# Load of a value unit's second half, issued by ScalarE instead of SyncE

## The chip, the cores and the metric

One core of a Trainium2 chip. The time is the device time of one execution in microseconds (us), as median of the runs shown; lower is better.

## The reference

One decoder layer on x of 256 rows by 1024 columns, float32, with two kinds of attention side by side:

```python
h = rms_norm(x, norm_pre_g)
proj = einsum('bsd,de->bse', h, w_in)        # w_in: 1024 x (8 * 512 + 8)
q_a, k_a, v_a, g_a, f_a, q_b, k_b, v_b, g_b = split(proj)
y_a = merge_heads(fox_attention(q_a, k_a, v_a, log_sigmoid(f_a + b))) * silu(g_a)
y_b = merge_heads(moba_attention(q_b, k_b, v_b, slopes)) * silu(g_b)
y = einsum('bse,ed->bsd', concatenate([y_a, y_b]), w_out)
out = x + rms_norm(y, norm_post_g)
```

Each kind has 8 heads of 64. `fox_attention` adds a bias from the running sum of the forget gates (`f_a`) to its causal logits; `moba_attention`, with one block for 256 rows, is causal attention with a slope by distance.

## The kernel before

**Precision.** Every float32 operand of a large product is split into two parts that TensorE multiplies in its `fp32r` form: ScalarE writes the high part (a copy rounded to `fp32r`), VectorE the low part (the difference). A product is three passes, high by high, high by low and low by high (`PASSES`, `V_PASSES`).

**Weights** come in units of 128 rows by 1024 columns, 512 KB. `RING = 4` of them have room in `raw` (as loaded) and in `w` (high and low). Units 0 to 7 are value units: unit u is one block of 128 input columns against all 1024 value columns, half of them (`va`) from one array unit and half (`vb`) from another, plus 8 forget columns that GpSimd copies in from `wf` (line 289). Units 8 to 15 are gate units, then queries and keys in turn. The rounding of a unit is `unit_high` (line 380, ScalarE) and `unit_low` (line 615, VectorE); its products are line 947 for values and 937 for the others. Gate unit `V_UNITS + s` waits for its low part and, from `s = 2`, for the gate product (line 680, VectorE) of the unit two before it, whose PSUM bank it takes.

**The beginning.** To let TensorE start early, the first three value units are cut (`PIECES`): unit 0 into columns 0 to 256, 256 to 512, 512 to 768 and 768 to 1032, units 1 and 2 into two halves. Each piece is rounded (line 411), its low part made (line 633) and multiplied on its own. The loads of unit 0 are three: 0 to 256 and 256 to 512 with 128 KB each, and 512 to 1024 with 256 KB, which lands for the last two pieces and is counted by the semaphore `s_raw_in[0]`. TensorE does eight products on ones (line 986) until the first piece is there. x comes transposed in column blocks (`x_t`, line 208), multiplied with `g_pre` and split by lines 398 (ScalarE) and 622 (VectorE).

**Who issues.** SyncE issues nearly all loads, in one order, on its DMA queue (q1 in the trace): x block 0, the three loads of unit 0, x block 1, the two halves of unit 1, then x block and unit for units 2 and 3; from unit 4 on each load first waits until the unit that had its place in the ring is rounded (`sp.wait_ge(s_lo, ...)`). Ahead of units 6 and 7, where no x block is left, x comes once more by rows (line 244, `x_rows`, in the tile named `h`), for the mean squares (line 394, ScalarE): two blocks of 128 rows. From them come `ms`, `root`, `rstd` (lines 424, 640 to 647), a load of another activation table (line 425) and the rounding of units 7 on. ScalarE's own DMA queue (q10) has few transfers; at the start `g_pre` (4 KB, line 387) and `w_f` (32 KB, line 390).

```python
for c, (lo, hi) in enumerate(X_LOADS):
    act.wait_ge(s_x_in[c], 16)
    for j in range(lo, hi):
        x_high(j)
    if c < PIECED:
        for lo, hi in PIECES[c]:
            last = hi == V_WIDTH
            act.wait_ge(s_raw_in[c] if lo >= HALF or c == 2 else s_piece_in[2 * c + lo // SEQ], 16)
            if last:
                act.wait_ge(s_wf, c + 1)
```

Of the kernel before, what the change touches and what calls it, by code (L numbers as in the profile page):

```python
# [27 lines left out]
D_MODEL = 1024  # L28
# [7 lines left out]
HALF = D_MODEL // 2  # L36
UNIT = 1024
V_UNITS = KT
# [25 lines left out]
def hybrid_layer(nc, xt, x, g_pre, w_units, w_f, f_bias, w_out, g_post, out):  # L64
    ctx = ExitStack()

    def sb(name, shape, dt=F32):
        return ctx.enter_context(nc.sbuf_tensor(name, shape, dt))

    def sem(name):  # L70
        return ctx.enter_context(nc.semaphore(name))
# [4 lines left out]
    with ctx:  # L76
# [10 lines left out]
        raw = sb("raw", [P, RING, V_PITCH])  # L87
# [71 lines left out]
        s_raw_in = [sem(f"raw_in{s}") for s in range(RING)]  # L159
# [43 lines left out]
        @block.sync  # L203
        def _(sp):

            def load_x(c):
                lo, hi = X_LOADS[c]
                sp.dma_start(x_t[:, lo:hi, :], xt[:, lo:hi, :]).then_inc(s_x_in[c], 16)

            def load_values(u, lo, hi, landed):  # L210

                part = slice(u % 2 * HALF + lo % HALF, u % 2 * HALF + (hi - 1) % HALF + 1)
                units = slice(lo // HALF * (V_UNITS // 2) + u // 2, V_UNITS, V_UNITS // 2)
                n = 1 if hi <= HALF else 2 - lo // HALF
                sp.dma_start(raw[:, u % RING, lo:hi].rearrange("p (a c) -> p a c", a=n),
                             w_units[units, :, part][0:n].rearrange("a p c -> p a c")).then_inc(landed, 16)

            load_x(0)
            load_values(0, 0, SEQ, s_piece_in[0])
            load_values(0, SEQ, HALF, s_piece_in[1])  # L220
            load_values(0, HALF, D_MODEL, s_raw_in[0])
            load_x(1)
            load_values(1, 0, HALF, s_piece_in[2])
            load_values(1, HALF, D_MODEL, s_raw_in[1])
            for u in range(2, RING):
                load_x(u)
                load_values(u, 0, D_MODEL, s_raw_in[u])

            def load_unit(r, s):

                sp.wait_ge(s_lo, r * RING + s + 1 - RING)
                sp.dma_start(raw[:, s, 0:UNIT], w_units[r * RING + s]).then_inc(s_raw_in[s], 16)

            def load_out_unit(j):
                if j > 1:
                    sp.wait_ge(s_olo, j - 1)
                sp.dma_start(raw_out[j % 2], w_out[j]).then_inc(s_raw_out_in[j % 2], 16)

            for u in range(RING, V_UNITS):
                if u < len(X_LOADS):  # L240
                    load_x(u)
                else:
                    t = u - len(X_LOADS)
                    sp.dma_start(x_rows[:, t, :], x[:, t, :]).then_inc(s_xrows_in[t], 16)
                sp.wait_ge(s_lo, u + 1 - RING)
                load_values(u, 0, D_MODEL, s_raw_in[u % RING])
            sp.dma_start(fb_row[:, :], f_bias.rearrange("h o -> o h").to_broadcast((P, HEADS))).then_inc(s_fb_in, 16)

            for u in range(V_UNITS, QK_0 + 2 * RING):
                load_unit(u // RING, u % RING)  # L250
                if u in OUT_BEHIND:
                    load_out_unit(OUT_BEHIND.index(u))


            for i in range(1, PAIRS + 1):
                for u in range(QK_0 + 6 + 2 * i, QK_0 + 8 + 2 * i):
                    if u < UNITS:
                        load_unit(u // RING, u % RING)
                    elif u < UNITS + RING:
                        sp.wait_ge(s_lo, u + 1 - RING)  # L260
                        sp.dma_start(raw[:, u % RING, 0:UNIT], w_out[OUT_OWN + u - UNITS]).then_inc(s_raw_in[u % RING], 16)
            sp.wait_ge(s_olo, OUT_OWN)
            sp.dma_start(gpost_row[:, :], g_post[0:1, :].to_broadcast((P, D_MODEL))).then_inc(s_gpost_in, 16)
            sp.wait_ge(s_h32, KT)
            sp.dma_start(x_nat, x).then_inc(s_xnat_in, 16)
            for t, c in ((0, 0), (0, 1), (1, 0)):
                sp.wait_ge(s_fin[t][c], 1)
                sp.dma_start(out[t, :, c * HALF:(c + 1) * HALF],
                             x_nat[:, t, c * HALF:(c + 1) * HALF]).then_inc(s_stored, 16)
            sp.wait_ge(s_last, 1)  # L270
            sp.dma_start(out[1, :, HALF + SEQ:], x_nat[:, 1, HALF + SEQ:]).then_inc(s_stored, 16)
            sp.wait_ge(s_stored, 16 * (2 * TT + 1))
# [100 lines left out]
        def _(act):  # L373
# [11 lines left out]


            act.dma_start(gpre_col[:, :], g_pre).then_inc(s_g_in, 16)
            act.wait_ge(s_ones, 1)
            nc.scalar.activation(root[:, 0:1], ones[:, 0:1], ACT.Sqrt).then_inc(s_table, 1)
            act.dma_start(wf[:, :, :], w_f).then_inc(s_wf_in, 16)  # L390
# [821 lines left out]
```

## Time and profile before

| | |
|---|---|
| runs | 144.88, 145.12, 145.19 us, median 145.12 |
| profiled execution | 145.13 us |
| its span, first to last instruction | 143.3 us |
| granted TensorE clock, mean | 0.992 |
| busy: TensorE, VectorE, ScalarE, GpSimd | 94%, 76%, 69%, 28% of the span |
| DMA moved | 26.96 MB, 188 GB/s over the span |

The profile is of one execution. Its time stands beside its span, since 1.8 us lie around the first and last instruction. Engines: PE is TensorE, PEld its weight loads, DVE VectorE, ACT ScalarE, POOL GpSimd, SP SyncE; a q behind the name (SPq, ACTq) is the engine's instruction queue, which issues DMAs. A share of busy time is a mean over stages with different limits: what one wait costs has to be read at its place.

### The profile page before, as it was taken

To read this page: it belongs to the slowest core of one execution; us is meant where nothing else is said; L and a number is where in the kernel's file an instruction comes from. 1 tells how busy PE (TensorE), PEld (TensorE's weight loads), DVE (VectorE), ACT (ScalarE), POOL (GpSimd) and SP (SyncE) were. 2 spreads that over 40 slices of the span, in tenths; PEclk is the share of its full clock that TensorE was granted. 3 is DMA by queue.
4 is the path that set the end of the run, shared out by engine and by line. 5 is a ranking of instruction groups with operands and counts; after the bars stand their busy time and mean duration, and the time that the engine had idled before them with its cause. 6 is when DMAs were issued, how large, how long until landed. Compare 5 with 4: busy or idle time off the path is not lost.

```text
span 143.3 us, 2857 instructions
## 1 busy us (share of the span) xinstructions
PE 134.4 (94%) x1076; PEld 127.4 (89%) x1076; DVE 109.4 (76%) x230; ACT 98.7 (69%) x198; POOL 40.0 (28%) x58
## 2 busy tenths in 40 slices
PE   7789999999999999999999999999999999999910
PEld 7679999999999999999999999999998888988910
DVE  0384966899999999988888977999689816471891
ACT  4376989678976398977875977778879833355740
POOL 3621100000000067000599235230735551120042
PEclk9999999999999999999999999999999999999996
DMA  4999999398865999758368603449600000000034
GB/s 110 233 313 386 401 395 342 88 375 254 271 223 172 389 392 377 278 160 238 112 230 237 213 9 142 146 166 293 280 2 0 0 0 5 0 0 0 0 149 146
DMA packets 9725, 26.96 MB, mean 188 GB/s; under 512 B 1384, under 2 KB 2416, under 8 KB 9456
## 3 DMA queue, kind: packets, MB, share of 16 engines
q1 hardware_dynamic: 9120, 25.57, 52.0%
q10 hardware_dynamic: 592, 1.22, 2.3%
q8 instruction: 8, 0.13, 0.4%
q14 instruction: 5, 0.04, 0.1%
HBM read 25.73 MB, written 1.06 MB: 187 GB/s over the span
## 4 chain that ended last, share of the span: by engine, by line
PE 87%; DMA 4%; issue 2%; DVE 2%; ACT 1%; POOL 1%; SPq 1%; POOLq 1%; DVEq 0%; ACTq 0%
PE bank L937 47%; PE score_banks L947 11%; PE bank L1128 7%; PE score_banks L1128 5%; PE score_banks L1033 4%; PE value_banks L947 4%; DMA raw<-in_w_units 4%; PE value_banks L1056 1%; PE value_banks L1044 1%; PE value_banks L1060 1%; PE value_banks L1045 1%; POOL x_t L366 1%; DVE h L882 1%; PE bank L1046 1%; PE value_banks L1059 1%
## 5 line engine op out<-in xcount | busy, mean ns | idle before, releaser
L615 DVE TENSOR_TENSOR w_lo<-raw,w_hi 128x1024 fp32r<-128x1024 f32 (+1 forms) x33 | 44.6, 1353 | 6.6 <-ACT w_hi L380 6.5
L380 ACT ACTIVATE w_hi<-raw 128x1024 fp32r<-128x1024 f32 (+1 forms) x33 | 34.4, 1056 | 6.5 <-DMA raw<-in_w_units 4.1
L937 PE MATMUL bank<-h_hi,w_hi 128*128 128x256 f32 x128 | 36.0, 281 | 0.0
L937 PE MATMUL bank<-h_lo,w_hi 128*128 128x256 f32 x128 | 35.6, 278 | 0.0
L937 PE MATMUL bank<-h_hi,w_lo 128*128 128x256 f32 x128 | 35.5, 278 | 0.0
L937 PEld LDWEIGHTS bank<-h_hi,w_hi 128*128 128x128 f32 x128 | 24.1, 188 | 0.4
L937 PEld LDWEIGHTS bank<-h_lo,w_hi 128*128 128x128 f32 x128 | 24.0, 188 | 0.0
L937 PEld LDWEIGHTS bank<-h_hi,w_lo 128*128 128x128 f32 x128 | 24.0, 188 | 0.0
L334 POOL TENSOR_TENSOR probs<-probs,row_inv 128x256 f32<-128x256 f32 (+1 forms) x16 | 15.7, 1005 | 27.6 <-DVE row_inv L764 27.5
L937 PE MATMUL bank<-xg_hi,w_hi 128*128 128x256 f32 x64 | 17.8, 278 | 0.0
L937 PE MATMUL bank<-xg_lo,w_hi 128*128 128x256 f32 x64 | 17.7, 277 | 0.0
L937 PE MATMUL bank<-xg_hi,w_lo 128*128 128x256 f32 x64 | 17.7, 276 | 0.0
L326 POOL TENSOR_TENSOR bias<-squares,causal 128x256 f32<-128x256 f32 x4 | 6.3, 1573 | 35.1 <-DMA squares<-decay_rows_scratch 35.1
L477 ACT ACTIVATE probs<-probs,neg_max 128x128 f32<-128x128 f32 (+1 forms) x32 | 14.1, 448 | 0.3 <-DVE neg_max L757 0.3
L937 PEld LDWEIGHTS bank<-xg_hi,w_hi 128*128 128x128 f32 x64 | 12.0, 188 | 0.0
L937 PEld LDWEIGHTS bank<-xg_lo,w_hi 128*128 128x128 f32 x64 | 12.0, 188 | 0.0
L937 PEld LDWEIGHTS bank<-xg_hi,w_lo 128*128 128x128 f32 x64 | 12.0, 188 | 0.0
L947 PE MATMUL score_banks<-w_hi,xg_hi 128*128 128x512 f32 (+2 forms) x34 | 8.8, 336 | 1.4 <-ACT w_hi L411 1.4
L947 PE MATMUL score_banks<-w_lo,xg_hi 128*128 128x512 f32 (+2 forms) x34 | 8.7, 330 | 0.0
L339 POOL TENSOR_TENSOR xg_lo<-y_parts,xg_hi 128x512 fp32r<-128x512 f32 x3 | 5.3, 1772 | 11.6 <-ACT xg_hi L488 11.6
L947 PE MATMUL score_banks<-w_hi,xg_lo 128*128 128x512 f32 (+2 forms) x34 | 8.5, 328 | 0.0
L947 PEld LDWEIGHTS score_banks<-w_hi,xg_hi 128*128 128x128 f32 x34 | 5.8, 188 | 2.0 <-ACT w_hi L411 1.6
(172 smaller groups left out, 326.5 us busy)
## 6 DMA issues: line engine op xcount, KB each, us to landing
raw<-in_w_units SPq DMA_DIRECT2D x30, 512.0 KB, 4.8
raw<-in_w_out SPq DMA_DIRECT2D x4, 512.0 KB, 3.2
h<-in_x SPq DMA_DIRECT2D x2, 512.0 KB, 8.1
y_parts<-in_w_out SPq DMA_DIRECT2D x2, 512.0 KB, 5.6
gpost_row<-in_w_out SPq DMA_DIRECT2D x2, 512.0 KB, 6.1
squares<-decay_rows_scratch ACTq DMA_DIRECT2D x1, 1024.0 KB, 5.9
x_t<-in_x SPq DMA_DIRECT2D x1, 1024.0 KB, 7.1
raw<-in_w_units SPq DMA_DIRECT2D x3, 256.0 KB, 5.2
```

What stands on the lines that cost most here:

```text
L326: pool.tensor_tensor(bias[:, own, :], decay[:, heads, 0:P], mask, ALU.add).then_inc(s_bias, 1)
L334: pool.tensor_tensor(own, own, row_inv[:, 4 * b + t:4 * b + 4:2].unsqueeze(2).to_broadcast((P, 2, hi - lo)), ALU.mult).then_inc(s_norm, 1)
L339: pool.tensor_tensor(y[1][:, 2 * d:2 * d + 2, :], y32[:, :, :], y[0][:, 2 * d:2 * d + 2, :].bitcast(F32), ALU.subtract).then_inc(s_ylo, 1)
L366: pool.tensor_tensor(x_nat[:, 0, HALF:], x_nat[:, 0, HALF:], y_post[:, 0, HALF:], ALU.add).then_inc(s_fin[0][1], 1)
L380: nc.scalar.activation(w[0][:, s, 0:width], raw[:, s, 0:width], ACT.Copy).then_inc(s_hi, 1)
L477: nc.scalar.activation(own, own, ACT.Exp, bias=neg_max[:, c:c + 1], scale=-1.0, accum_out=row_sum[:, c:c + 1]).then_inc(s_exp, 1)
L615: nc.vector.tensor_tensor(w[1][:, s, 0:width], raw[:, s, 0:width], w[0][:, s, 0:width].bitcast(F32), ALU.subtract).then_inc(s_lo, 1)
L882: nc.vector.tensor_tensor(kept, group, gpost_row[:, cols], ALU.mult).then_inc(s_ypost, 1)
L937: last = nc.tensor.matmul(dst, stationary(a, j), moving(b, j), start=n == 1, stop=n == count * len(PASSES))
L947: last = nc.tensor.matmul(v_banks[t][c][:, lo - first:hi - first], xg[a][:, u, t * P:(t + 1) * P], w[b][:, u % RING, lo:hi], start=u == 0 ...
L1033: last = nc.tensor.matmul(s_ps[:, 2 * (i % 2) + a, lo:hi], q[x][own, i % 4, t * P:(t + 1) * P], k[z][own, i % 2, 0:hi - lo], start=n == 0, ...
L1128: last = nc.tensor.matmul(dst, y[a][:, p, t * P:(t + 1) * P], wide, start=p == 0 and (a, b) == PASSES[0], stop=p == PAIRS - 1 and (a, b) = ...
```

## The change

The load of columns 512 to 1024 of value unit 0 leaves SyncE's list and stands in ScalarE's program, directly behind `g_pre`'s. Source, destination and semaphore stay the same.

```diff
@@ -218,7 +218,6 @@
             load_x(0)
             load_values(0, 0, SEQ, s_piece_in[0])
             load_values(0, SEQ, HALF, s_piece_in[1])
-            load_values(0, HALF, D_MODEL, s_raw_in[0])
             load_x(1)
             load_values(1, 0, HALF, s_piece_in[2])
             load_values(1, HALF, D_MODEL, s_raw_in[1])
@@ -385,6 +384,7 @@
 
 
             act.dma_start(gpre_col[:, :], g_pre).then_inc(s_g_in, 16)
+            act.dma_start(raw[:, 0, HALF:D_MODEL], w_units[V_UNITS // 2, :, 0:HALF]).then_inc(s_raw_in[0], 16)
             act.wait_ge(s_ones, 1)
             nc.scalar.activation(root[:, 0:1], ones[:, 0:1], ACT.Sqrt).then_inc(s_table, 1)
             act.dma_start(wf[:, :, :], w_f).then_inc(s_wf_in, 16)
```

SyncE's first instructions, before (`raw` is the ring of weights, 128x256 and 128x512 are pieces of it; `x_t` is transposed x):

```order
L208 DMA x_t<-in_xt 128x256
L215 DMA raw<-in_w_units 128x256 x2
L215 DMA raw<-in_w_units 128x512
L208 DMA x_t<-in_xt 128x256
L215 DMA raw<-in_w_units 128x512 x2
```

and with the change:

```order
L208 DMA x_t<-in_xt 128x256
L215 DMA raw<-in_w_units 128x256 x2
L208 DMA x_t<-in_xt 128x256
L215 DMA raw<-in_w_units 128x512 x2
```

One load is gone from between the two small pieces and x's second block. ScalarE's first instructions, before (`root<-ones` is the activation that brings the first table):

```order
L387 DMA gpre_col<-in_g_pre 128x8
L389 ACT_TABLE_LOAD
L389 ACTIVATE root<-ones 128x1
L390 DMA wf<-in_w_f 128x64
L398 ACTIVATE xg_hi<-x_t,gpre_col 128x256
```

and with the change (a line less in the code above moves `g_pre` to line 386):

```order
L386 DMA gpre_col<-in_g_pre 128x8
L387 DMA raw<-in_w_units 128x512
L389 ACT_TABLE_LOAD
L389 ACTIVATE root<-ones 128x1
L390 DMA wf<-in_w_f 128x64
L398 ACTIVATE xg_hi<-x_t,gpre_col 128x256
```

The load stands between `g_pre`'s and the table load, and ahead of `w_f`'s on the same queue. TensorE, VectorE and GpSimd keep their instructions and order.

## Rows read from the trace of the kernel before

**Rows 1.** Waits of TensorE: engine, line, waited for: us, times, longest.

```profile
PE score_banks L947 <- ACT w_hi L411: 1.4, 1, 1.4
PE bank L986 <- POOL ones L291: 1.0, 1, 1.0
```

**Rows 2.** Chain of waits, 0 to 40 us: start, us, what.

```profile
0.75 0.38 SPq L208
1.19 0.42 SPq L215
1.66 0.42 SPq L215
2.12 5.16 DMA raw<-in_w_units
7.31 0.42 ACT w_hi L411
7.78 0.38 PE score_banks L947
```

**Rows 3.** Timeline, 0 to 14 us: start, us, engine, line, what [idle before, ended by].

```profile
1.20 1.28 ACT L389 ACT_TABLE_LOAD   x1 [1.20 <-PEq L1205]
...
3.71 0.51 ACT L398 ACTIVATE xg_hi<-x_t,gpre_col 128x256 fp32r<-128x256 f32 x1 [1.02 <-DMA gpre_col<-in_g_pre]
...
4.21 0.99 POOL L289 COPY raw<-wf 128x8 f32<-128x8 f32 x4 [2.34 <-DMA wf<-in_w_f]
...
6.01 0.40 PE L947 MATMUL score_banks<-w_lo,xg_hi 128*128 128x256 f32 x2
...
7.78 0.38 PE L947 MATMUL score_banks<-w_hi,xg_hi 128*128 128x256 f32 x1 [1.36 <-ACT w_hi L411]
...
8.34 1.26 ACT L411 ACTIVATE w_hi<-raw 128x512 fp32r<-128x512 f32 x2
...
9.31 0.63 PE L947 MATMUL score_banks<-w_hi,xg_hi 128*128 128x512 f32 x2
```

**Rows 4.** DMA, first 3.5 us: packets by queue; issues, count, KB each, us to landing.

```profile
q1 hardware_dynamic: 371, 0.34, 33.2%
q10 hardware_dynamic: 277, 0.03, 6.4%
...
raw<-in_w_units SPq DMA_DIRECT2D x2, 128.0 KB, 2.8
wf<-in_w_f ACTq DMA_DIRECT2D x1, 32.0 KB, 2.9
```

**Rows 5.** Windows: us, busy of PE, PEld, DVE, ACT, POOL, clock, DMA share, GB/s.

```profile
2.00:4.00 2.00, 2.00 (x12) 2.00 (x11) 0.00 (x0) 0.97 (x3) 0.00 (x0) 1.00 0.79 205
4.00:6.00 2.00, 2.00 (x14) 1.82 (x14) 1.15 (x3) 0.83 (x3) 1.74 (x14) 1.00 0.89 213
6.00:8.00 2.00, 0.64 (x6) 0.43 (x4) 0.24 (x1) 0.69 (x3) 0.67 (x3) 1.00 0.96 285
8.00:14.00 6.00, 6.00 (x40) 5.46 (x40) 4.40 (x9) 4.08 (x9) 1.18 (x3) 1.00 1.01 359
14.00:21.50 7.50, 7.50 (x52) 6.91 (x51) 5.52 (x8) 6.51 (x11) 0.38 (x1) 1.00 1.05 398
25.48:46.60 21.12, 21.12 (x179) 20.75 (x179) 20.98 (x38) 15.80 (x22) 0.00 (x0) 1.00 0.70 232
```

**Rows 6.** Timeline at unit 3, 13 to 15 us.

```profile
13.48 1.07 ACT L380 ACTIVATE w_hi<-raw 128x1032 fp32r<-128x1032 f32 x1 [1.14 <-DMA raw<-in_w_units]
...
14.96 0.39 PE L947 MATMUL score_banks<-w_hi,xg_hi 128*128 128x512 f32 x1
```

**Rows 7.** Timeline, ScalarE, VectorE and TensorE, 21 to 41 us.

```profile
21.48 1.06 ACT L394 ACTIVATE squares<-h 128x1024 f32<-128x1024 f32 x1 [0.26 <-DMA h<-in_x]
...
25.48 2.37 DVE L615 TENSOR_TENSOR w_lo<-raw,w_hi 128x1032 fp32r<-128x1032 f32 x2 [0.90 <-ACT w_hi L380]
...
29.53 0.28 PE L937 MATMUL bank<-xg_hi,w_hi 128*128 128x256 f32 x1
...
37.08 0.42 DVE L680 TENSOR_TENSOR gate<-bank,rrow 128x256 f32<-128x256 f32 x1
...
39.68 0.42 DVE L680 TENSOR_TENSOR gate<-bank,rrow 128x256 f32<-128x256 f32 x1
...
40.43 0.38 PE L1016 MATMUL score_banks<-ident,forget 128*8 128x128 f32 x2
40.56 0.37 PE L937 MATMUL bank<-xg_hi,w_hi 128*128 128x256 f32 x1
```

**Rows 8.** DMA, issue at 13.2 us: KB, us to landing.

```profile
h<-in_x SPq DMA_DIRECT2D x1, 512.0 KB, 8.3
```

## The prediction

> **What bounds the kernel now.** I read the waits of TensorE first, since it is busy for 94% of the span. It has two idle stretches in the whole program [rows 1]: 1.0 us at the start, before anything can run, and 1.4 us for ScalarE's `w_hi`, the high half of a weight. Everything else on TensorE follows back to back, and what stands behind its last product is a fixed tail. So the change can give at most those 1.36 us, and only as far as nothing later takes them back.
>
> The chain of waits shows where the 1.36 us come from [rows 2]. SyncE issues x's first column block and then three pieces of value unit 0. The third, its second half (512 columns, 256 KB), is issued at 2.12 and has landed 5.16 us later, at 7.28. ScalarE rounds it from 7.31, TensorE starts on it at 7.78. The timeline [rows 3] shows the two sides of the hole: the last product of the first two pieces begins at 6.01, and the one at 7.78 has an idle time of 1.36 before it.
>
> **What the change does to that load.** ScalarE's queue now holds `g_pre` (issue 0.75), the half, and `w_f`. `g_pre`'s issue ends and ScalarE's table load starts at 1.20 [rows 3], so the half is issued at about 1.2 instead of 2.12: 0.9 earlier. SyncE loses one issue of 0.46 (its issues follow each other at that distance, 1.19, 1.66, 2.12) [rows 2], so x's second block and all that follows is issued 0.46 earlier.
>
> When does the half land? Upper bound: it takes 5.16 again, 6.4. Lower bound: 2.8, as a 128 KB piece just ahead of it took [rows 4], 4.0; it is larger and shares the engines with the others, so I take 5.7, between them. Either way TensorE, done with the first pieces near 6.4, could go on by 6.9 at the latest (6.4, plus 0.42 of ScalarE and 0.1 of hand-over). So **up to 0.9 to 1.36 us are offered here**.
>
> **What pays for it.** (a) x's first block and the first two pieces share the DMA engines with 256 KB more. At the full rate of [rows 5], 398 GB/s, those are 0.66 us. TensorE would finish the first pieces at 7.1 at worst, which is inside the hole: nothing. (b) The activation table load moves from 1.20 to 1.65. ScalarE waits 1.02 us for `g_pre` behind it [rows 3], so nothing. (c) `w_f` now comes behind 256 KB in one queue. It landed 2.9 after its issue; now it lands with the half. GpSimd needs 0.25 for the first of four copies (0.99 together) [rows 3], ScalarE 0.32 for the third piece before it wants them: 0 to 0.1. GpSimd's later work moves back by as much as `w_f` (4.2 to about 5.8, 1.6 us); its next copies are wanted for units 2, 3 and 4, the first of them by ScalarE at about 11 and unit 3's at 13.48 [rows 6]. The copies for units 0 to 3 are one run of 0.99, so this is hidden too.
>
> **What takes it back.** This decides the size. Next to be late are things that the DMA engines deliver, not what the moved load frees.
>
> Unit 1: its first half is rounded from 8.34 in two activations of 1.26 together, so the first is ready at 8.97; TensorE uses it at 9.31 [rows 3]. Room: 0.34, less 0.05 of hand-over (rounding ends at 7.73, product at 7.78), 0.29.
>
> Unit 3: rounded from 13.48 to 14.55 directly on its landing, used at 14.96 [rows 6]. Room 0.41 - 0.05 = 0.36.
>
> Gate unit 11 (the fourth): four gate units run from 29.53 to 40.43, so 2.72 each, and the fourth starts at 37.70. It waits for two VectorE steps, the low half of its weight and the gate product of unit 9. That product runs at 37.08 and ends at 37.50 [rows 7]. Room 0.20 - 0.05 = **0.15**. VectorE is busy for 20.98 of the 21.12 us from 25.48 on [rows 5], so this time isn't set by TensorE but by when VectorE began. That was set by ScalarE's table load and the rounding of unit 7, behind the square sums of x's second row block, which started on a landing (idle 0.26, "DMA h<-in_x") at 21.48 [rows 7]. The fifth gate unit has 0.46 - 0.05 = 0.41 in the same way (product ends at 40.10, used at 40.56) [rows 7].
>
> So TensorE can gain no more than 0.15 plus what the landing of x's second row block is pulled forward; call that d. The DMA engines' share [rows 5] bounds d. From 8 us on they are full (1.01, 1.05): an earlier issue there is worth nothing, since x's second row block takes 8.3 us from issue to landing anyway [rows 8]. Only time in which they idled can be won: in 2 to 4 us the share is 0.79, so 0.42 us idle, about SyncE's 0.46 of issue time. Upper end d = 0.42. Lower end d = 0, if the slowest of the sixteen engines, which sets each landing, had no idle time. Below that it could fall, because the share counts slow packets as work: 213 GB/s at a share of 0.89 in 4 to 6 us, against 398 at 1.05 later. Nothing in the trace says that a second queue makes those better or worse. I take d = 0.2, the middle.
>
> **Sum.** Gain 0.15 + 0.2 = 0.35 us, the other 0.55 or more turning into short waits of TensorE at unit 1, unit 3 or the gates. The profiled execution took 145.13, the median is 145.12, so nothing is corrected: **144.8 us**. About 0.2% (0.29 us) is what a measurement can tell from no change.
>
> Does a second queue add anything? The rows show the two queues' packets side by side in the first 3.5 us (371 of q1, 277 of q10) [rows 4]. The Trainium skill, "DMA: Bandwidth & Descriptors", section "Issuing engines are not separate DMA queues", says that DMAs started from different engines run on the same 16 DMA engines and interleave, so that only the sequencer's time to start them is saved. The trace agrees as far as it goes. By that rule, where the engines are full, the sum would be 0.15 alone.
>
> **Rivals.**
>
> 1. *No pull-in (d near 0).* The half lands early, but every later landing keeps its time since the bytes ahead are the same. For: the shares of 1.01 and 1.05 [rows 5] and the 8.3 us [rows 8]. Against: the 0.79 at the start. TensorE starts early and gives all but 0.15 back at gate unit 11: 144.97, within noise. This is also what the rule of the Trainium skill gives.
> 2. *More than that.* The slow packets of 4 to 6 us overlap across two queues. 213 GB/s instead of the 285 of the next two microseconds leaves 0.14 MB behind, 0.4 us at 359 GB/s. Then d = 0.2 + 0.4, gain 0.75, 144.4. Unit 1 and unit 3 must be pulled along.
> 3. *The other side.* Two queues taking turns prolong the slow phase, or push one engine further behind; x's second row block lands later. The price at 213 instead of 359 GB/s is 0.4 us for each microsecond that the slow phase grows. It decides from 0.15 us on, the room at gate unit 11. With 1.5 us of growth: d = -0.6, 0.45 slower, 145.6.
> 4. *The change doesn't do what it says.* The half is held up on the slow engines and lands at 7.3 as before, since it was not the issue but the packets that were late. For: 5.16 against 2.8 for an issue 0.46 before it. TensorE starts at 7.78: 145.1.
>
> **Chances.** Forecast (d from 0.14 to 0.42) 0.45; rival 1 (d within 0.14 of zero, gain 0.01 to 0.29) 0.32; rival 2 0.08; rival 3 0.10; rival 4 0.05. Faster by over 0.2% are forecast and rival 2, less what touches the bound: 0.50. Within: rivals 1 and 4 and the small end of 3: 0.41. Slower: 0.09. Range: from rival 2, 144.3, over forecast and rival 1 to a small case of rival 3, 145.3. The forecast's own range, d from 0.14 to 0.42, is 144.55 to 144.85.
>
> **What would show it.** The half's landing before 6.5, and the hole before its first product at 0.5 us or less. New short waits of TensorE, for ScalarE at unit 1 or 3, or for VectorE at the fourth gate unit, 0.5 us or more in sum. x's second row block starting its squares at about 21.3 instead of 21.48, and VectorE's run at 25.3 instead of 25.48. The prediction is wrong if that squares row moves by more than 0.5 either way, if TensorE has no new wait although it began a microsecond earlier, or if the first pieces' products end after 7.8. If squares and run move but the time doesn't, it is the argument on gate unit 11 that failed.

## The result and the profile after

| | before | with the change |
|---|---|---|
| median of 22 runs each | 145.31 us | 146.76 us |
| ratio, 95% interval | | 1.0055, 1.0033 to 1.0078 |
| profiled execution, its span | 145.13, 143.3 | 146.74, 144.9 |

The change makes the kernel slower, by 0.55% (0.33% to 0.78%), where 0.35 us faster was forecast. The ratios, here and below, leave out executions of over 1.5% above a kernel's fastest, 10 of 22 with the change and 2 of 22 before, which is why the medians are further apart (1.45 us, 1.0%) than this ratio. Each ratio below is against executions of the kernel before taken beside that version; their medians are 145.16 to 145.33.

The waits of TensorE in the changed kernel name the same pair as [rows 1], 0.4 us longer:

```profile
PE score_banks L947 <- ACT w_hi L411: 1.8, 1, 1.8
PE bank L986 <- POOL ones L290: 1.0, 1, 1.0
```

But it is another hole. The chain of waits, against [rows 2]:

```profile
0.75 0.38 SPq L208
1.18 4.82 DMA raw<-in_w_units
6.03 0.43 ACT w_hi L411
...
6.59 3.11 PE score_banks L947 x13
```

The load in the chain is no longer the one that was moved, it is SyncE's second: value unit 0's **first piece**, 128 KB, issued at 1.18 as ever and landed at 6.00 instead of 3.99. (3.99 is the earliest of four traces with SyncE's old list: in those of experiments 2 and 7, where only the number of products on ones differs, it is 4.53, 4.67 and 4.82. So the piece is 1.2 to 2.0 us later.) The moved half did land earlier, at about 6.6 instead of 7.3 (issue 1.20, 5.4 us), but nobody waits for it. The timeline, against [rows 3]:

```profile
6.03 0.42 ACT L411 ACTIVATE w_hi<-raw 128x256 fp32r<-128x256 f32 x1 [2.21 <-DMA raw<-in_w_units]
...
6.59 0.77 PE L947 MATMUL score_banks<-w_hi,xg_hi 128*128 128x256 f32 x2 [1.81 <-ACT w_hi L411]
...
7.15 1.04 POOL L288 COPY raw<-wf 128x8 f32<-128x8 f32 x4 [5.28 <-DMA wf<-in_w_f]
7.15 0.63 PE L947 MATMUL score_banks<-w_hi,xg_lo 128*128 128x256 f32 x2
...
7.58 0.63 PE L947 MATMUL score_banks<-w_lo,xg_hi 128*128 128x256 f32 x2
...
8.00 0.63 PE L947 MATMUL score_banks<-w_hi,xg_hi 128*128 128x256 f32 x2
...
10.22 0.28 PE L947 MATMUL score_banks<-w_hi,xg_hi 128*128 128x264 f32 x1
...
10.34 0.28 PE L947 MATMUL value_banks<-w_hi,xg_hi 128*128 128x264 f32 x1
...
10.95 0.62 PE L947 MATMUL score_banks<-w_hi,xg_hi 128*128 128x512 f32 x2
```

Two things are to be seen. The hole of 1.36 ahead of the half is gone, and one of 1.81 stands ahead of the first product, which begins at 6.59, not 4.67. And from 7.15 on, pairs of products of 256 columns follow each other every 0.43, so 0.213 each; from 9.9 on it is 0.12, TensorE's usual pace here. 256 columns in 0.213 us are one column per cycle at 1.2 GHz, the lower of the clock's two levels. The views print a granted clock of 1.00 for this stretch, but the trace has no record of the clock before 9.77: there the first one begins, and it is of the upper level, 2.4 GHz. In the kernel before, the first record begins at 4.43, while TensorE is still at the products on ones. So in this trace TensorE went into its real work at the lower level, and 1.00 printed ahead of the first record says nothing. Thirteen such steps lie between 6.94 and 9.71 (three in the kernel before) and cost 1.2 us. Unit 1 begins at 10.95 instead of 9.31, 1.64 later, and the execution takes 1.61 more. The first gate product, at 29.53 before [rows 7], is at

```profile
31.15 0.28 PE L937 MATMUL bank<-xg_hi,w_hi 128*128 128x256 f32 x1
```

From there to the end of the execution it takes 115.6 us in both kernels (145.13 - 29.53, 146.74 - 31.15), and 115.50 to 115.77 in all 20 traces. So all but 0.3 us of any difference is made before it.

The windows, against [rows 5]:

```profile
2.00:4.00 2.00, 2.00 (x12) 2.00 (x11) 0.08 (x1) 1.67 (x3) 0.00 (x0) 1.00 0.77 158
4.00:6.00 2.00, 0.78 (x4) 0.48 (x3) 0.41 (x1) 0.00 (x0) 0.00 (x0) 1.00 0.85 258
6.00:8.00 2.00, 1.41 (x6) 1.44 (x7) 1.05 (x3) 1.49 (x5) 0.85 (x4) 1.00 1.03 350
```

158 GB/s in 2 to 4 us instead of 205, at nearly the same share of busy time. The phase of slow packets, in which the engines are busy and deliver little, is not longer than before; it has moved forward. Before, it lay behind the first pieces (213 GB/s in 4 to 6). Now it lies on them, as it comes with the half.

### The profile page after: what moved, and what is told of

Read it like the earlier page. It is cut to its first block, busy times and chain, and to the rows that moved or that the text cites. A ratio compares the mean times of both kernels' runs of the same rounds, so it can differ in the third digit from the quotient of the medians.

```text
span 144.9 us, 2857 instructions
## 1 busy us (share of the span) xinstructions
PE 135.6 (94%) x1076; PEld 128.7 (89%) x1076; DVE 109.8 (76%) x230; ACT 98.6 (68%) x198; POOL 41.2 (28%) x58
## 4 chain that ended last, share of the span: by engine, by line
PE 88%; DMA 3%; issue 2%; DVE 2%; ACT 1%; POOL 1%; POOLq 1%; SPq 0%; DVEq 0%; ACTq 0%
PE bank L937 46%; PE score_banks L947 13%; PE bank L1128 7%; PE score_banks L1128 5%; PE score_banks L1033 4%; PE value_banks L947 4%; DMA raw<-in_w_units 3%; PE value_banks L1056 1%; PE value_banks L1044 1%; PE value_banks L1060 1%; PE value_banks L1045 1%; POOL x_t L365 1%; DVE h L882 1%; PE bank L1046 1%; PE value_banks L1059 1%
## 5 line engine op out<-in xcount | busy, mean ns | idle before, releaser
L325 POOL TENSOR_TENSOR bias<-squares,causal 128x256 f32<-128x256 f32 x4 | 6.9, 1737 | 36.7 <-DMA squares<-decay_rows_scratch 36.7
L947 PE MATMUL score_banks<-w_hi,xg_hi 128*128 128x512 f32 (+2 forms) x34 | 9.4, 354 | 1.8 <-ACT w_hi L411 1.8
L947 PE MATMUL score_banks<-w_hi,xg_lo 128*128 128x512 f32 (+2 forms) x34 | 9.0, 345 | 0.0
L947 PEld LDWEIGHTS score_banks<-w_hi,xg_hi 128*128 128x128 f32 x34 | 6.3, 208 | 2.4 <-issue 2.1
```

Of the source, the lines that this page charges most:

```text
L325: pool.tensor_tensor(bias[:, own, :], decay[:, heads, 0:P], mask, ALU.add).then_inc(s_bias, 1)
L947: last = nc.tensor.matmul(v_banks[t][c][:, lo - first:hi - first], xg[a][:, u, t * P:(t + 1) * P], w[b][:, u % RING, lo:hi], start=u == 0 ...
```

## Experiments

**1. A second trace of the change.**

> The changed kernel once more, as a second trace. Theory F (the first piece pays): value unit 0's first piece, which landed at 3.99 before and at 6.00 in the changed kernel's trace, lands late again, above 5.0; TensorE's hole stands ahead of line 947's first product, and behind a hole of over about 1.5 us its products of 256 columns follow each other at 0.21 us instead of 0.12 for some 3 us. Time 145.5 to 147. Rival N (chance): the first trace caught an odd execution, the slow packets at 2.9 to 3.9 us are not the change's, and here the first piece lands by 4.5 and the time is 145.2 or less.

Median 146.02, ratio 1.0038 (1.0006 to 1.0071), profiled 145.75. The first piece lands at 6.09, the half at 6.86, so theory F is right on the landing. On the pace it is not: the products keep 0.12 behind a hole of 1.89, and the record of the upper clock level begins at 5.49, ahead of them:

```profile
6.67 0.47 PE L947 MATMUL score_banks<-w_hi,xg_hi 128*128 128x256 f32 x2 [1.89 <-ACT w_hi L411]
6.99 0.40 PE L947 MATMUL score_banks<-w_hi,xg_lo 128*128 128x256 f32 x2
7.22 0.40 PE L947 MATMUL score_banks<-w_lo,xg_hi 128*128 128x256 f32 x2
```

This splits the 1.61 us of the first trace: 0.6 for the late first piece (145.75 against 145.13; the first product comes 2.0 later and the hole of 1.36 is gone), 1.0 for the half pace, which this execution did not have. How many of the others had it isn't known, since only two were traced.

**2. Longer warm-up.** `-WARM_UP = 8` `+WARM_UP = 14`, on the changed kernel and on the one before.

> The changed kernel with 14 instead of 8 products on ones, so that TensorE is busy until about 6.2. Theory F with the clock: the first piece lands as late as in the changed kernel (5 to 6), but its products run at 0.12 from the start, so that unit 1 begins about 1.4 us earlier than in the changed kernel: time within 0.3 of the kernel before. Rival L (only the late landing costs, the pace of the products is not the hole's doing): the time is that of the changed kernel, 146 to 146.8, or later by what the products on ones overrun.

> The control: the kernel before with 14 products on ones. They end near 6.1 instead of 4.67 and delay the first two pieces, whose products (1.4 us at the fast pace) then end near 7.6, still ahead of the second half's first product at 7.78. Both theories: no change, 145.0 to 145.5. If it is slower by more than 0.3, the products on ones cost by themselves and the run above has to be read against this one.

Medians 145.61 (ratio 1.0027, 1.0010 to 1.0044) and 145.51 (1.0025, 1.0006 to 1.0044). The products on ones ran to 7.16 and 7.07, later than the 6.2 I had written: I had taken them to double their pace early, and they keep 0.21 until the upper clock level is on record, from 6.84 and 6.66 (the last of them are 0.11 apart). So they overran the first piece in both (first product at 6.92 and 6.83), no hole is left, and with it the two kernels are alike, though the first piece lands at 5.86 in one and 4.53 in the other. The changed kernel's spread shrinks from 144.8 to 148.8 to 145.1 to 145.9 (one of 230 us left out). The late landing alone, with TensorE kept busy until it, costs nothing that shows.

**3. The contention alone.** In the kernel before:

```diff
             act.dma_start(gpre_col[:, :], g_pre).then_inc(s_g_in, 16)
+            act.dma_start(gate[:, 0:2, :].rearrange("p a n -> p (a n)"), w_units[V_UNITS // 2, :, 0:HALF]).then_inc(s_extra, 16)
...
+            dve.wait_ge(s_extra, 16)
             gate_product(V_UNITS)
```

> The kernel before, with its second half loaded by SyncE as ever, and the same 256 KB loaded a second time by ScalarE behind g_pre's load into a tile that is not in use yet (the extra data is used for nothing). It measures the contention alone. Theory F: the first piece lands at 5 to 6 as in the changed kernel although SyncE's list is untouched, and the time is at least that of the changed kernel, 146 to 148 (0.25 MB more ahead of all others is 0.66 us at 398 GB/s). Rival S (the changed kernel is late because SyncE's later loads start 0.46 earlier and crowd the first pieces, not because of ScalarE's load): the first piece lands near 4.0 and the time is 145.1 to 145.8.

Median 146.97, ratio 1.0064 (1.0024 to 1.0104); first piece at 6.15. SyncE's list is that of the kernel before, so its earlier issues are not to blame. Rival S falls. This trace also shows the half pace beside a clock record. The products are 0.21 apart from 7.68 to 11.11, and the granted clock, last but two in the row, is at 0.50, the lower level:

```profile
7.70:11.10 3.40, 3.40 (x17) 3.40 (x17) 3.04 (x7) 2.69 (x6) 3.18 (x16) 0.50 1.04 384
```

Here the upper level was on record from 4.25, and it fell at 7.66: TensorE had been idle from 4.58 to 6.74 and busy again for 0.9 us.

**4. The same bytes ahead, on SyncE's own queue.** `load_values(0, HALF, D_MODEL, s_raw_in[0])` moved up, behind `load_x(0)`.

> The second half on SyncE's queue as before, but ahead of the first two pieces, so that the same bytes are in front of them with no second queue. Theory B (bytes and slow packets: whatever stands in front of or beside the first piece delays it): the first piece lands at 5.0 to 6.2, as in the changed kernel (6.0), and the time is 145.6 to 147. Rival Q (two queues taking turns are what is slow): the first piece is late only by the 256 KB at 398 GB/s and one issue, 0.66 + 0.46, so at about 5.1 or below with no packets of over 0.3 us in front, and the time stays within 0.4 of the kernel before.

Median 146.46, ratio 1.0059 (1.0016 to 1.0103). Half at 4.70, first piece at 5.78, a hole of 1.58. It isn't the second queue: one queue makes the first piece as late. But the profiled execution took 145.03, no longer than the kernel before's: its upper clock level is on record from 4.82 and no product is at half pace. Three of the ten took 144.9 to 145.1, five 146.4 to 147.0. So a late first piece of itself costs between nothing (here) and 0.6 us (experiment 1).

**5. Other moments for the moved load.** Behind `w_f`'s issue, and behind the wait for `g_pre`.

> The changed kernel with the second half issued behind w_f's load instead of ahead of it (about 1.6 instead of 1.2). Theory B: its packets start some 0.4 us later, the first piece has fewer of them beside it and lands at 4.5 to 5.5, the second one still late; hole ahead of the first piece under 1.5 us, time 145.2 to 146.2, between the two kernels. Rival (any load on the second queue does it): first piece at 6.0 and 146 to 146.8 as in the changed kernel.

> The second half issued by ScalarE only when g_pre has landed (about 3.3), 1.2 us later than SyncE issued it before. Theory B: the first two pieces land at 4.0 and 4.4 as before; the half now competes with x's second block and unit 1 and lands at 7.0 to 8.0; TensorE's hole of 1.4 us stays ahead of the half; time 145.0 to 145.8. Rival: if a queue of its own got the half through in 2.8 us, it would land by 6.2 and the time would be 144.7 to 144.9.

Behind `w_f`: first piece at 4.36, earlier than theory B had it, second piece at 6.25 (4.36 before), half at 6.79, median 145.09, ratio 0.9971 (0.9941 to 1.0001). 0.5 us later at the issue, and the slow packets lie behind the first piece again; most of the loss is gone, though a gain is not certain: eight executions took 144.2 to 145.5, four 146.6 to 147.1. Behind the landing: 147.51, ratio 1.0164 (1.0121 to 1.0206), slower than either theory said, for the half takes 6.2 us and lands at 9.55, with everything else ahead of it or beside it:

```profile
10.04 0.39 PE L947 MATMUL score_banks<-w_hi,xg_hi 128*128 128x256 f32 x1 [3.55 <-ACT w_hi L411]
```

Here a queue of its own gave the load no precedence. The next products follow at 0.12: the upper clock level is on record from 4.85 and stays, even through a hole of 3.55.

**6. The second piece moved instead.** Of the kernel before, `load_values(0, SEQ, HALF, s_piece_in[1])` goes to ScalarE's queue behind `g_pre`, the half stays.

> A version that might beat both: of the kernel before, the second piece (128 KB) goes to ScalarE's queue behind g_pre, the half stays on SyncE's and is issued 0.46 earlier. Theory B: half of the changed kernel's bytes beside the first piece and of 1 KB packets as its own: first piece at 4.3 to 5.2 (hidden up to about 4.4, then TensorE is idle ahead of it), half at 6.8 to 7.3; time 144.8 to 145.5. If the first piece lands at 6, the second queue is to blame at any size.

Median 144.98, ratio 0.9982 (0.9942 to 1.0021): no change that can be told, but its profiled execution is the fastest of the lot, 144.23. First piece at 4.51, half at 6.30. The half came earlier than expected. At the fourth gate unit, where the prediction put its limit, the square sums start at 20.58 (21.48 before), the gate product ends at 36.60, 16.02 later in both kernels, and is used at 36.77:

```profile
36.18 0.42 DVE L680 TENSOR_TENSOR gate<-bank,rrow 128x256 f32<-128x256 f32 x1
...
36.77 0.28 PE L937 MATMUL bank<-xg_hi,w_hi 128*128 128x256 f32 x1
```

TensorE and VectorE both come 0.9 us earlier, so the room stays, 0.17 against 0.20 [rows 7], and the limit isn't reached. But the prediction's upper end for d, 0.42, isn't a general bound: with another load moved the square sums come 0.90 earlier.

**7. The hole without the late landing, and two warm-ups.** `WARM_UP = 4` and `10` in the kernel before, `10` in the version of experiment 6.

> The kernel before with 4 instead of 8 products on ones: they end near 2.9, so TensorE is idle for 1.8 us ahead of the first piece, as in the changed kernel, but every load lands as before. Theory C (such a hole costs by itself, because TensorE's products behind it often run at half pace): landings unchanged (4.0, 7.3), products of 256 columns 0.21 apart for some 2 to 3 us in part of the executions, the runs spread to over 146.5, median 0.3 to 1.2 above the kernel before. Rival (only the landing matters, the first pieces are ready at 4.6 anyway): 145.0 to 145.4, spread as before.

> Control for it: the kernel before with 10 products on ones. They end near 5.4, the first pieces' near 6.8, the hole ahead of the half shrinks from 1.4 to 0.9 to 1.0 us and the half's products start at 7.8 as ever: median within 0.2 of the kernel before. By theory C its slower executions (over 146) become rarer.

> The version with the second piece (not the half) on ScalarE's queue, with 10 products on ones instead of 8. They end near 5.4, the first pieces' products (1.4 us) near 6.8, which is when the half's began in that version's trace (6.80): no hole of over 0.3 us is left. Theory C: no executions with a half pace, so the spread goes and the median is 144.2 to 144.8. Rival: 145.0 with a spread of over 1.5 us as without them.

With 4: median 146.08, ratio 1.0037 (0.9999 to 1.0075), products at half pace from 5.60 to 9.68 in its trace, where the first piece landed at 4.67 and the hole was 2.18; the upper clock level is on record from 9.78 only. Landing, pace, median and spread (to 147.65) are what theory C expected, though the interval of the ratio still touches 1. With 10: 145.60, ratio 1.0012 (0.9973 to 1.0052), three of 12 runs over 146, which is no rarer than without (9 of 35). The second piece with 10: 145.21, ratio 0.998 (0.9944 to 1.0016), spread 1.5, but its half landed at 6.57 and left a hole of 0.73, so it doesn't test what it was meant to. A hole without a late landing can bring the half pace, then; that every long hole does is refuted by experiments 1, 4 and 5.

**8. Which rows are read.** The extra load of experiment 3 again, then with other sources: `w_units[V_UNITS // 2 + 1, :, 0:HALF]` (array unit 5) and `w_out[PAIRS - 1, :, 0:HALF]`.

> As the kernel before with the extra 256 KB load on ScalarE's queue, but its source is w_out's last unit (rows of 4 KB pitch, the same packets of 2 KB) instead of the rows of value unit 0's second half. If the slow packets come from beginning to read those rows of the value weights while the first pieces' are read, the first piece lands at 4.3 to 5.0 and the time is 145.2 to 146. If any 256 KB beside the first pieces brings them, the first piece lands at 5.8 to 6.3 and the time is 146 to 147 as with the first extra load.

> The first extra load (the half's own rows, 256 KB, on ScalarE's queue, the half itself still on SyncE's) once more, on the same chip as the three below. First piece at 5.8 to 6.3 again, 146 to 147. If it lands below 5, the difference to w_out's rows was one of chips or executions.

> The same extra load with rows of array unit 5 instead of 4: 2.5 MB instead of 2 MB behind the rows of the first pieces, same pitch and packet size. Theory A (rows exactly 2 MB apart, read side by side, are what makes the packets slow): first piece at 4.5 to 5.2, as with w_out's rows (4.87), and few packets over 0.25 us between 3 and 4.5 us (5, against 19 with unit 4). Theory V (any rows of that array beside the first pieces): 5.8 or later.

> The extra load from w_out's last unit once more. First piece at 4.6 to 5.2 again. If it lands at 5.8 or later here, its first trace was luck, and bytes beside the first pieces are enough.

From `w_out`'s rows the first piece lands at 4.87 and, again, at 4.56, about where most traces of the kernel before have it (4.53 to 4.82); from unit 4's at 6.15 and 5.72, from unit 5's at 5.65. The issue of the first piece (KB, us to landing) and the window of 3 to 4.5 us, unit 4:

```profile
raw<-in_w_units SPq DMA_DIRECT2D x1, 128.0 KB, 4.5
...
3.00:4.50 1.50, 1.40 (x9) 1.20 (x7) 0.49 (x1) 0.68 (x2) 0.00 (x0) 1.00 0.91 165
```

unit 5:

```profile
3.00:4.50 1.50, 1.50 (x9) 1.49 (x7) 0.48 (x1) 0.68 (x2) 0.00 (x0) 1.00 1.01 185
```

and `w_out`:

```profile
raw<-in_w_units SPq DMA_DIRECT2D x1, 128.0 KB, 3.4
...
3.00:4.50 1.50, 1.50 (x9) 1.49 (x7) 0.48 (x1) 0.68 (x2) 0.00 (x0) 1.00 0.89 310
```

310 GB/s against 165 and 185, for the same 256 KB in the same packets (282 and 177 in the first traces of the two). Theory A as written (exactly 2 MB apart) falls with unit 5; theory V stands for these loads: rows of another unit of the same array beside unit 0's are slow, another array's are not. The times, with 4 to 12 runs each, do not separate these four: 146.97 and 147.07 (unit 4), 146.49 (unit 5), 145.74 and 146.44 (`w_out`), the last two apart by as much as the sources are.

The last of these traces is also the one in which the limit of the prediction acts. The gate product that the fourth gate unit waits for ends at 37.37, and that unit starts 0.05 later:

```profile
36.95 0.41 DVE L682 TENSOR_TENSOR gate<-bank,rrow 128x256 f32<-128x256 f32 x1
...
37.42 0.39 PE L940 MATMUL bank<-xg_hi,w_hi 128*128 128x256 f32 x1
```

TensorE loses 0.15 us there (its products, else 0.11 apart, start at 37.28, 37.42 and 37.65), and from the first gate product to the end it takes 115.77 instead of 115.60.

**9. The changed kernel, the half from an array of its own.** The launch lays a copy of that unit into `w_copy`:

```diff
-            act.dma_start(raw[:, 0, HALF:D_MODEL], w_units[V_UNITS // 2, :, 0:HALF]).then_inc(s_raw_in[0], 16)
+            act.dma_start(raw[:, 0, HALF:D_MODEL], w_copy[:, 0:HALF]).then_inc(s_raw_in[0], 16)
```

> The changed kernel, its second half read from an array of its own that holds a copy of that unit (same pitch of 4 KB, another address). Theory A: the first piece lands at 4.6 to 5.2 instead of 6.0, the half by 5.5 to 6.0; TensorE begins near 5.2 and the time is 144.6 to 145.3 where its products keep their pace. Theory V, or bytes alone: first piece at 6.0, time 145.7 to 146.8 as in the changed kernel.

Median **144.64, ratio 0.9961 (0.9932 to 0.9990)**: faster than the kernel before, with the same move that made it slower. (Eight of 12 executions took 143.9 to 144.8, four 145.7 to 146.3.)

```profile
raw<-in_w_copy ACTq DMA_DIRECT2D x1, 256.0 KB, 4.4
raw<-in_w_units SPq DMA_DIRECT2D x1, 128.0 KB, 4.2
...
3.00:4.50 1.50, 1.50 (x9) 1.47 (x7) 0.48 (x1) 0.68 (x2) 0.00 (x0) 1.00 0.83 289
...
5.99 0.47 PE L947 MATMUL score_banks<-w_hi,xg_hi 128*128 128x256 f32 x2 [1.33 <-ACT w_hi L411]
```

The half lands at 5.62, the first piece at 5.41 (later than the 5.2 expected; it is 4.48 in experiment 10, with the same loads), and the rest is delivered in time: unit 1's first product is at 8.91 instead of 9.31. A further array may also shift where the others lie in memory; that was not looked at.

**10. The own array without the move, and with 11 products on ones.**

> The kernel before, its half read from the array of its own, on SyncE's queue as before. Theory A2 (what is slow is reading two places of the weights' array at once): the half lands earlier than at 7.3, at 5.3 to 6.5, the first piece at 4.0 to 4.5, TensorE's hole of 1.4 shrinks to under 0.5, and the gain is the 0.3 to 0.6 that units 1 and 3 allow: 144.5 to 144.9. If it stays at 145.0 to 145.3, the own array helps only where two queues read side by side, and the moved issue is what brings the 144.64 of the version before.

> The changed kernel with the own array and 11 products on ones, which end near 5.7 instead of 4.7, so that little or no hole is left ahead of the first piece (ready at 5.0 to 6.0). Theory C: the slower executions (over 145.7, 4 of 12 without) go, since they are those whose products run at half pace; median 144.3 to 144.7, spread under 1.2. Rival: the same 144.6 with the same spread, or later by what the products on ones overrun.

Without the move: median 145.78, ratio 1.0021 (0.9994 to 1.0049), not the gain that theory A2 expected. The half lands at 5.70, within its bounds, and TensorE's holes are elsewhere:

```profile
5.21 0.47 PE L947 MATMUL score_banks<-w_hi,xg_hi 128*128 128x256 f32 x2 [0.43 <-ACT w_hi L411]
8.89 0.70 PE L947 MATMUL score_banks<-w_hi,xg_hi 128*128 128x512 f32 x2 [0.59 <-ACT w_hi L411]
10.85 0.39 PE L947 MATMUL score_banks<-w_hi,xg_hi 128*128 128x256 f32 x1 [0.33 <-ACT w_hi L411]
```

The slow phase has moved once more, to unit 1, whose two halves now land at 8.09 and 10.14 (8.28 and 8.94 before): the second of them is the first load that reads array unit 4. In 6.5 to 8 us the engines deliver 102 GB/s (289 before), at a busy share of 0.41:

```profile
6.50:8.00 1.50, 1.50 (x15) 1.50 (x14) 0.88 (x3) 0.36 (x1) 1.13 (x4) 1.00 0.41 102
```

A share of 0.41 is unlike the slow stretches shown so far (0.77 to 1.01): here the engines have few packets in flight. In experiment 9 the same two loads of the same rows land at 7.96 and 8.60, with 280 GB/s in that window. So in these runs the gain took both, the array and the move, and why unit 1 is spared there is open. With 11 products on ones: 144.86, ratio 0.9970 (0.9946 to 0.9994), spread 144.4 to 145.7 instead of 143.9 to 146.3: about as fast (144.3 to 144.7 was expected) and, over 12 runs each, steadier. In its trace there is no hole, and yet

```profile
5.71 0.77 PE L947 MATMUL score_banks<-w_hi,xg_hi 128*128 128x256 f32 x2
6.29 0.63 PE L947 MATMUL score_banks<-w_hi,xg_lo 128*128 128x256 f32 x2
6.71 0.53 PE L947 MATMUL score_banks<-w_lo,xg_hi 128*128 128x256 f32 x2
```

from 6.07 to 6.92 the products are 0.21 apart, directly behind the products on ones. The upper clock level is on record from 6.99. The half pace does not need a hole.

## Why the prediction was wrong

**What bounds the kernel, and what the change offers: right in the main.** The hole of 1.36 us was the half's, the half is issued at 1.20, and in both traces of the change it lands earlier (6.56 and 6.86, forecast 5.7, bounds 4.0 and 6.4, so later than the upper one).

**Part (a) of what pays for it: the step that failed.** It said that the 256 KB beside the first pieces cost 0.66 us at 398 GB/s, that TensorE would finish the first pieces at 7.1 at worst, and that this is free. They cost 1.2 to 2.0 us on the first piece (5.86 to 6.09 in three traces, against 3.99 to 4.82 in four), and TensorE *begins* the first pieces at 6.6. I priced the bytes at the rate of 14 to 21 us, while [rows 5] had 205 to 213 GB/s for just this stretch, and 5.16 us for the half itself against 2.8 for its neighbour [rows 2, 4]. I used both rows, the one to bound d and the other to place the half's landing, and not to ask what the slow packets would do to what stands beside the half. Experiments 3 and 4 show that step alone: the load added or put ahead, 5.7 to 6.2 for the first piece, on either queue. Experiment 8 shows that the bytes alone aren't it: with as many of `w_out`'s rows the first piece (4.87, 4.56) is about where three of the four traces of the kernel before have it (4.53 to 4.82). It goes with the half's rows lying in the array from which the first pieces are read; why those are slow stays open.

**The clock: missing.** No term of the sum had it. In the profiled execution TensorE is at the lower level until 9.77, which costs 1.2 us; in experiment 1 it is at the upper one from 5.49, and the late piece alone costs 0.6. That the late start matters for it is borne out by experiment 2, where without a hole the two kernels are alike (145.61 and 145.51).

**(b) and (c): right.** The table load and GpSimd's copies ended nothing that was waited for: the copies ran from 7.15, and ScalarE wanted the first after its third piece, some 0.3 later. `w_f` itself was later than forecast, at 7.09 and not with a half at 5.7.

**What takes it back: not reached, so not tested here.** d was forecast as 0.2 with ends 0 and 0.42; the square sums of x's second row block start at

```profile
21.20 1.06 ACT L394 ACTIVATE squares<-h 128x1024 f32<-128x1024 f32 x1 [0.21 <-DMA h<-in_x]
```

0.28 earlier. That is no more than chance: it is 21.43 in experiment 1, and 21.08 to 21.63 in the kernel before with 4, 10 and 14 products on ones. In the changed kernel TensorE came 1.6 us late to all of it. That the limit at the fourth gate unit is real, with its hand-over of 0.05, is shown by one trace of experiment 8; that d is 0.42 at most doesn't hold for every move: in experiment 6 it is 0.90, or 0.50 against the earliest trace of the kernel before.

**The rivals.** Rival 3 had the right side and the wrong mechanism: two queues taking turns and x's row block late, deciding from 0.15 at gate unit 11. The block came early; the price was paid at the first product. Its 145.6 and the range's 145.3 were too low. Of the signs I had named, "the first pieces' products end after 7.8" is the one that came true.

**The rule on queues.** The Trainium skill, "DMA: Bandwidth & Descriptors", section "Issuing engines are not separate DMA queues", was cited for a sum of 0.15. The trace agrees with its main part (84 packets of q10 among 116 of q1 in 3 to 4.5 us, and experiment 4 is as slow on one queue); beside that, the load that gains those 0.9 us of issue takes them, and more, from the loads beside it (first piece 1.2 to 2.0 us later).

## What to carry to other kernels

A load that is started earlier is paid for by those that were in front of it, so price it on the first one that somebody waits for, and at the rate that the engines deliver in that stretch, not at their best. Where a stretch is busy but slow, find out which reads make it slow before anything is moved into it. Take more than one trace of the kernel before, too: its first piece landed anywhere from 3.99 to 4.82. Here the same move costs 0.55% with the data in one array and gains 0.39% (0.10% to 0.68%) with a 512 KB copy of one unit in another. One profiled execution showed 1.6 us; a second one showed 0.6: where a stretch of TensorE at half pace is in the trace, look at more, and look for where the first clock record begins.

## What the runs showed of the hardware

- **Slow packets, early in the program, go with which rows are read.** In 3 to 4.5 us the engines delivered 145 to 185 GB/s when 256 KB of a second unit of `w_units` were read on ScalarE's queue beside unit 0, 282 to 310 when they came from another array (the changed kernel and experiments 1 to 3 against 8, 9 and 10; unit 5 and a repeat are in 8). The phase moved with the half (experiments 4 and 5) and, in one version with the half gone to an array of its own, to the next load of that unit (experiment 10), in another not (experiment 9). It isn't all: in experiment 5, behind the landing, 3 to 4.5 us has 197 GB/s though the half's first packet starts at 5.76. And it passes: the loads of the later value units, each of which reads two units of the array at once, come at 398 GB/s in 14 to 21.5 us [rows 5]. Whether it is the array, or distances that are multiples of 512 KB as those of all its units are, was not tried.
- **TensorE at the lower clock level** (0.213 us for 256 columns) for 1.3 to 4.5 us of its real work was in 7 of 20 traces, all in the first 12 us. In each the stretch ends where a record of the upper level begins. In five that is the first record, at 9.77 (the changed kernel), 9.78 (four products on ones), 9.61 (the first extra load from `w_out`), 6.57 (behind `w_f`) and 6.99 (own array, 11 products on ones); the views print 1.00 ahead of it. In two, both traces of the first extra load, the clock had been at the upper level from 4.25 and 3.85, fell at 7.66 and 7.26 behind holes of 2.2 and 1.9, and was back at 11.07 and 10.68. In the other 13 it was at the upper level from 3.96 to 6.84, by the first product, and stayed there through holes of up to 3.55. The Trainium skill, "TensorE: Matmul & The Clock Gate", section "Part 1: The HAM clock gate", has an idle engine fall to 1.2 GHz, busy time release it, and the same kernel differ between executions by the phase at which it starts. The difference between executions agrees: with the same program and the products on ones done at 4.78 in both, the changed kernel was released at 9.77 in one trace and at 5.49, while idle, in the other. A rule by the hole's length alone doesn't. What decides it in one execution stays open.
